# Forgetting attention as one unrolled pipeline over all heads, with keys and values turned to token order inside the input projection

## The reference, cut to what matters

```python
q, k, v, lf, xq, gate = split_fox(rmsnorm(x) @ fox_w_in, b_f)     # (2048, 8, 128) each of q, k, v
c = cumsum(lf)                                                    # per head, over tokens
s = (q_i @ k.T) * 128**-0.5 + (c_i[:, None] - c_keys[None, :])    # one block of 128 queries, causal
p = softmax(s); out = p @ v                                       # then out * silu(gate)
fox_k_prompt, fox_v_prompt = k, v in pages of 128 tokens: (16, 128, 8, 128)
```

## Time and profile before

| what | value |
|---|---|
| times of three runs | 3939.87, 3943.66, 3946.54 us |
| the profiled execution | 3935.28 us, its span 3933.8 us |
| mean granted PE clock | 0.95 of full speed |
| PE, PEld, DVE, ACT, POOL busy | 90%, 78%, 48%, 34%, 9% |
| `p00` (48 to 640 us) | 592 us |
| `p01` (640 to 1633 us) | 993 us |
| `prompt_gates` (1633 to 1662 us) | 29 us |
| `fox_attention` (1662 to 2444 us) | 782 us |
| output projection and layer 1 (2444 us on) | 1490 us |

### The profile page before, as it was taken

The page is one execution under the profiler, slowest core; times in us unless marked ns, Lnnn a source line. Parts: engine busy times, 40 slices in busy tenths (PEclk is TensorE's granted clock), DMA queues, the critical chain, the costliest instruction groups (busy, mean ns, idle before and its releaser), DMA issues. The chain is left out here.

```text
span 3933.8 us, 56268 instructions
## 1 busy us (share of the span) xinstructions
PE 3527.3 (90%) x19825; PEld 3070.0 (78%) x19825; DVE 1887.2 (48%) x3394; ACT 1333.0 (34%) x2456; POOL 338.7 (9%) x549
## 2 busy tenths in 40 slices
PE   5999998899999999688888886899499889995999
PEld 5999997788888877577777776688499878774787
DVE  3332232466666645366666665433322245565432
ACT  3112222255555534355555553111212254310111
POOL 1320000011111101001001000000000001121000
PEclk8999999999999999899999998899699999997999
DMA  3444333577777653322222222333233343565332
GB/s 120 125 124 142 115 120 90 187 234 234 228 240 240 220 167 108 105 96 96 92 93 86 86 86 63 117 113 95 87 114 118 103 128 114 168 198 186 100 113 78
DMA packets 385338, 523.96 MB, mean 133 GB/s; under 512 B 52855, under 2 KB 275064, under 8 KB 380495
## 3 DMA queue, kind: packets, MB, share of 16 engines
q1 hardware_dynamic: 317255, 398.72, 32.4%
q0 software_dynamic: 30624, 93.22, 7.1%
q10 hardware_dynamic: 37248, 29.37, 2.5%
HBM read 388.83 MB, written 132.74 MB: 133 GB/s over the span
## 5 line engine op out<-in xcount | busy, mean ns | idle before, releaser
L395 ACT ACTIVATE z_st_p<-bank 128x352 f32<-128x352 f32 (+3 forms) x325 | 168.2, 519 | 728.0 <-PE bank L378 727.3
L1518 PE MATMUL bank<-w_hi_o,b_hi_o 128*128 128x512 f32 x816 | 328.6, 403 | 69.4 <-DVE w_lo_o L1560 69.4
L378 PE MATMUL bank<-h00hi,w_hi_p 128*128 128x352 f32 x984 | 320.7, 326 | 11.4 <-DVE w_lo_p L353 7.5
L1519 PE MATMUL bank<-w_hi_o,b_lo_o 128*128 128x512 f32 x816 | 324.4, 398 | 0.0
L1520 PE MATMUL bank<-w_lo_o,b_hi_o 128*128 128x512 f32 x816 | 324.3, 397 | 0.0
L378 PE MATMUL bank<-h00hi,w_lo_p 128*128 128x352 f32 x984 | 316.9, 322 | 0.0
L378 PE MATMUL bank<-h00lo,w_hi_p 128*128 128x352 f32 x984 | 316.8, 322 | 0.0
L351 DVE CAST w_hi_p<-w_raw_p 128x1024 fp32r<-128x1024 f32 (+1 forms) x130 | 89.8, 691 | 442.8 <-PE bank L378 383.6
L378 PE MATMUL bank<-h01hi,w_hi_p 128*128 128x512 f32 x656 | 270.0, 412 | 11.6 <-DVE w_lo_p L353 11.6
L378 PE MATMUL bank<-h01lo,w_hi_p 128*128 128x512 f32 x656 | 258.4, 394 | 0.0
L378 PE MATMUL bank<-h01hi,w_lo_p 128*128 128x512 f32 x656 | 258.2, 394 | 0.0
(11 more groups left out here) (354 smaller groups left out, 8788.2 us busy)
## 6 DMA issues: line engine op xcount, KB each, us to landing
z<-z_st_p SPq DMA_DIRECT2D x128, 512.0 KB, 2.9
k_raw_sf<-in_cache_fox_k SPq DMA_DIRECT2D x128, 512.0 KB, 4.1
v_raw_sf<-in_cache_fox_v POOLq DMA_DIRECT2D x128, 512.0 KB, 4.5
w_raw_p<-in_fox_w_in SPq DMA_DIRECT2D x80, 512.0 KB, 5.4
b_raw_o<-bT SPq DMA_DIRECT2D x32, 768.0 KB, 7.3
w_raw_p<-in_pool_w_in SPq DMA_DIRECT2D x48, 512.0 KB, 5.1
out<-tok_fa ACTq DMA_DIRECT2D x64, 256.0 KB, 2.3
w_raw_o<-in_w_out ACTq DMA_DIRECT2D x24, 512.0 KB, 3.6
```

What stands on the lines that cost most here:

```text
L378: last = nc.tensor.matmul(out, wt[:, u, k, :], h[:, k, at0:at0 + width], start=(m == 0), stop=(m == MM - 1))
L395: nc.scalar.activation(z_st[0:rows, t % 2, at0:at0 + width], banks[n % 2][0:rows, 0:width], func).then_inc(z_read, 1)
L1518: nc.tensor.matmul(out, bh, w_hi[:, k, cols], start=(k == 0), stop=False)
L1519: nc.tensor.matmul(out, bl, w_hi[:, k, cols], start=False, stop=False)
```

## The change: what it does

**In the projection's passes.** The tiles of k and v come ahead of those of q. A list of jobs replaces the plain order of chunks: after the first chunk of the tile that follows a k or v tile, PE transposes the rows of the k or v tile in `z_st` into the same two PSUM banks (two jobs of 4 transposes of 128 tokens each, in `p00` a third job of one transpose for the 32 sample tokens). ACT copies them to a new buffer `tok` (three in turn) and SP stores them to the outputs. The rows of v are no longer stored to `zT`. `sample_gates` loses its transposes, copies and stores.

**In the attention.** The hardware loop over heads is gone: one list of 128 steps (`NS_`) plus 7 runs through all heads, so that step 0 of a head is the step after step 15 of the one before. q, k and v are loaded in quarters of 512 tokens (v from the output in token order, in pieces of 512 bytes) into two raw buffers each, with k's and v's halves in two buffers. The halves of a quarter of the next head (`splits`) are made in steps x with x mod 4 = 0 (q), 1 (k), 2 (v): ACT makes the hi half after the exponential of that step, DVE the lo half after `nm` and the reciprocal. The set-up of a head, its 32 transposes and its stores are gone. `sc` has 3 buffers in place of 4. Product and spread inverse of pair J share bank 6 + J mod 2, so that two pairs have banks of their own. The spread is two float32r matmuls behind the product's last one, from `dg_hi` and `dg_lo`, which POOL makes in two further operations; POOL no longer stores, SP does.

```diff
-    NT, C, Q = len(tiles), len(chunks), 4
+    jobs = []
+    for t in range(NT):
+        for ch in range(C):
+            jobs.append((t, ch, None))
+            if ch == 0 and t and tiles[t - 1][4] is not None:
+                jobs += [(t - 1, None, part) for part in token_outs[0]]
...
         def _(pe):
+                u, bank = t % 2, banks[n % 2]
+                if q == 0 and n >= 2:
+                    pe.wait_ge(z_read, n - 1)
+                if part is not None:
+                    at0, count, width = part
+                    pe.wait_ge(z_read, tile_done[t])
+                    for b in range(count):
+                        last = nc.tensor.transpose(bank[0:width, b * P:(b + 1) * P], z_st[:, u, at0 + b * P:at0 + b * P + width],
+                                                   const["ident"][:, :])
+                    last.then_inc(z_done, 1)
+                    continue
...
             def evict(n):
+                act.wait_ge(z_done, n + 1)
+                if part is not None:
+                    nc.scalar.copy(tok[0:width, m % TR, 0:count, :], bank[0:width, 0:count * P]...).then_inc(z_read, 1)
+                    return
...
-            with pe.Fori(0, FH) as h:
-                for g in range(TG):
...
+        def splits(x):
+            if x < 0:
+                return [(n, 0, ch) for ch in range(CK) for n in range(3)] if x == -1 else []
+            out = []
+            for n in range(3):
+                h, rest = divmod(x - 4 - n, NQ)
+                if rest % 4 == 0 and 1 <= h + 1 < FH:
+                    out.append((n, h + 1, rest // 4))
+            return out
...
         def _(act):
+            for x, qs, qt, _, _, _ in steps():
+                if qt is not None:
+                    ... casts of the transposed pieces to pT_hi ...
+                if qs is not None:
+                    nc.scalar.activation(sc[:, qs % NB, 0:w], sc[:, qs % NB, 0:w], ACT.Exp, ...).then_inc(p_done, 1)
+                for n, h, ch in splits(x):
+                    split(n, h, ch)          # one cast of 128x512 to the hi half, then_inc(hi_d[n], 1)
...
         def _(dve):
+            def split(n, h, ch):
+                i = CK * h + ch
+                dve.wait_ge(hi_d[n], i + 1)
+                ... one operation of 128x512 for the lo half, then_inc(lo_d[n], 1)
+            for x, qs, qt, _, jr, jm in steps():
+                ... gate and mix (jm), decay, scores and lo halves by piece, nm, reciprocal (jr): the order of before
+                for n, h, ch in splits(x):
+                    split(n, h, ch)
...
         def _(pe):
+                            if n == QB * (j + 1) - 1:
+                                last.then_inc(o_done, 1)
+                                pe.wait_ge(dgl_d, J + 1)
+                                nc.tensor.matmul(OUT[J % 2][1], ones_r[:, :], dg_hi[:, :, :]..., start=True, stop=False)
+                                nc.tensor.matmul(OUT[J % 2][1], ones_r[:, :], dg_lo[:, :, :]..., start=False, stop=True).then_inc(r_done, 1)
```

More of the change, by code:

```diff
@@ L277, in stored @@
         def stored(t):
-            return 16 * len(stores) * (t // 2 + 1)
+            return 16 * len(stores) * sum(1 for x in range(t % 2, t + 1, 2) if tiles[x][1] is not None)
         def landed(eng, t):
@@ L320, in _ @@
                 beside.advance(at)
+            for m in waiting:
+                store_tokens(m)
             store(NT - 1)
@@ L323, in _ @@
             for t in (NT - 2, NT - 1):
-                sp.wait_ge(z_out[t % 2], stored(t))
+                if stored(t):
+                    sp.wait_ge(z_out[t % 2], stored(t))
+            for u in range(TR if turned else 0):
+                sp.wait_ge(tok_out[u], 16 * len(turned[u::TR]))
         @block.gpsimd
@@ L388, in evict @@
             def evict(n):
-                t, ch = divmod(n, C)
-                func, rows = tiles[t][2:]
+                t, ch, part = jobs[n]
+                bank = banks[n % 2]
+                act.wait_ge(z_done, n + 1)
+                if part is not None:
+                    _, count, width = part
+                    m = turned.index(n)
+                    if m >= TR:
+                        act.wait_ge(tok_out[m % TR], 16 * (m // TR))
+                    nc.scalar.copy(tok[0:width, m % TR, 0:count, :], bank[0:width, 0:count * P].rearrange("p (n d) -> p n d", d=P)).then_inc(z_read, 1)
+                    return
                 at0, width = chunks[ch]
-                act.wait_ge(z_done, n + 1)
-                if ch == 0 and t >= 2:
+                if ch == 0 and t >= 2 and stored(t - 2):
                     act.wait_ge(z_out[t % 2], stored(t - 2))
[L395 to L400, removed]
+                rows_t = tiles[t][3]
+                nc.scalar.activation(z_st[0:rows_t, t % 2, at0:at0 + width], bank[0:rows_t, 0:width], tiles[t][2]).then_inc(z_read, 1)
+            for n, t, ch, part, q, at in slots():
+                if q == 0 and n:
+                    evict(n - 1)
+                if part is None:
+                    beside.advance(at)
+            evict(len(jobs) - 1)
             beside.rest()
@@ L713, in _ @@
-            for n in range(4):
-                act.wait_ge(tok_out[n], 16 * 2 * FH + 1)
+            def split(n, h, ch):
+                i = CK * h + ch
+                act.wait_ge(raw_in[n][i % 2], 16 * (i // 2 + 1))
+                if n == 0 and h:
+                    act.wait_ge(s_done, first[NQ * (h - 1) + 4 * (ch + 1)])
+                if n == 1 and h >= 2:
+                    act.wait_ge(s_done, first[NQ * (h - 1)])
+                if n == 2 and h >= 2:
+                    act.wait_ge(o_done, NCH * (h - 1))
+                nc.scalar.activation(his[n][part(n, h, ch)], raws[n][:, i % 2, :], ACT.Copy, scale=SCALE if n == 0 else 1.0).then_inc(hi_d[n], 1)
```

623 lines of the change are left out of this document (305 added, 318 removed).

## The result

The changed kernel takes 3953.19 us, the median of 18 runs (3943.75 to 3962.28), against 3944.65 us of the kernel before in the same rounds (3937.45 to 3952.02). The ratio is 1.0023, 95% interval 1.0016 to 1.0031: slower, by 6 to 12 us. The forecast was +26. The direction was right and the size was not; so the question is which terms of the sum were off, since the net is a small difference of terms of up to 107 us.

What follows compares the result with a forecast made beforehand. PE was taken to bound the projection passes, a DVE-ACT chain of waits the attention. Terms +60 −105 −22 +99 −11 +5 gave +26 on the median 3943.7: 3969 us; 80% range 3912 to 4002, the forecast's own 3945 to 3990.

Steps and rivals of the forecast that it cites:

- (c): Waits in the attention's body: banks and diagonals ready, steps 4, 7, 8, 15 shorter, −2.8 us a head; −22 us.
- Unrolling itself I put at nothing: Attention's head loop: writing it out changes no time, since the projection's code has no loop and PE runs at 99%.
- (a): Projection passes: k and v transposes between chunks, PE waiting for ACT's copies out of two banks; +60 us.
- (b): Seven borders between heads, step 15 to step 3: 20.7 us in place of 35.7; −105 us.
- (d): Splits in the attention: DVE waits for ACT's hi half behind the exponential, 1.3 or 2.1 us each; +99 us.
- (f): SBUF ports in the attention: DVE's splits slowed beside POOL's operations after steps 4, 6 and 8; +5 us.
- (e): Ends of the attention stage: shorter start before the first nm, −5, and end after the last, −6; −11 us.
- Rival B: Projection passes: the transpose jobs cost only PE's own work, 27 us; 3937 us in all, chance 0.10.
- rival C: Passes: ACT's side work delays copies in most tiles, or token stores delay paged loads; +32, 4001 us, chance 0.15.
- 0.87 + E: Attention splits: time from nm to DVE's start of the lo half, E being the exponential's length.
- Rival A: Attention: DVE's wait is slack because PE sets the step, only ACT's cast is paid; 3904 us, chance 0.20.

Runs made afterwards that it cites:

- the last two experiments: Kernel before with its head loop written out on all engines: 3911.39 us, ratio 0.9911; the same without DVE's increment of an unawaited semaphore: 3912.2 us, ratio 0.9917.
- no_turn: Changed kernel without the token transposes and their copies, all stores kept (sending zeros): 3893.86 us, ratio 0.9873 to the kernel before.
- hi_first_one_bank: hi_first with one product bank for all pairs in place of two: 3895.17 us, ratio 0.9871 to the kernel before.
- hi_first: Changed kernel with ACT making a split's hi half before the exponential of its step: 3856.0 us, ratio 0.9773 to the kernel before.

## Why the prediction was wrong in size, step by step

The step that failed is the line "Unrolling itself I put at nothing", and with it the size of term (c). Unrolling alone takes 32 us off the kernel before, and together with an unneeded increment it explains steps 8 and 12, which the forecast had nearly unchanged.

| term | forecast | measured | from |
|---|---|---|---|
| (a) transposes in the passes | +60 | +65.5 | `p00` +43.0, `p01` +22.5 |
| (b) borders | −105 | −106.6 | 251.3 to 144.7 |
| (c) waits in the body | −22 | −30.6 | last head 55.8 against 59.6, times 8 |
| (d) splits, with (f) ports | +104 | +96.8 | 543.2 − 8 × 55.8 |
| (e) ends, with the output projection's start | −11 | −14 | table; output projection 377.4 to 375.3 |
| sum | +26 | +11 | |

The sum of the measured terms, +11, agrees with the median's +8.5 (6 to 12). Of the 15 us between it and the forecast, (c) makes 9, (d) and (f) 7, (e) 3 and (b) 2, and (a) takes 5 back. The mechanisms of (a), (b), (d) and (f) hold; that of (c) was incomplete. The other misses are sizes, 2 to 7 us a term, and the larger ones fell on one side.

*(a) held.* PE's waits are 2.05 us at a plain tile of `p00` (1.99 forecast) and 1.3 to 1.6 in most of `p01` (1.34), 2.3 and 1.8 at its last two. The two late tiles of `p00` took 4.7 and 6.6, 7.2 us more than two plain ones, where 7.4 had been added. Rival B (only PE's own transposes) and rival C (late copies in most tiles, or stores that hold up the paged loads) fall with no_turn and with those rows: ACT is late at two tiles of `p00`, and at none by more than about 1 us in `p01`.

*(b) held:* 20.7 forecast, 20.7 in all seven borders. Its chain holds too: product J = 7 starts 12.6 us after `nm` of step 15 in head 2, as forecast (11.7, and 0.9 for the quarters). Of the 106.6 us some 10 are the clock: in the kernel before a border took 34.5 us where PE's granted clock was 1.00 and 35.3 to 36.8 where it was 0.86 to 0.90; in the changed kernel it is 1.00 in all seven.

*(c) failed in size,* and with it the line "Unrolling itself I put at nothing". I had argued from the projection, whose code has no loop and whose PE is 99% busy. In the attention's loop the waits on registers stand in DVE's chain: unrolling alone takes 14 us out of steps 3 to 15 (462.7 against 477.0), 14 out of the borders (which the forecast had inside its 20.7) and 2 to 3 at the ends. In the changed kernel the body's gain is 0.54 at step 4, 1.9 at step 7, 0.44 at step 8, 0.35 at step 12, 0.28 at step 15 and 0.3 over the rest; I had counted 0.5, 1.7, 0.2, none, 0.3 and none. Steps 8 and 12 are settled by the last two experiments. Step 7's 1.9 has three parts. The forecast gave it to the diagonal, the clock and the bank. About 0.8 is the clock, which did fall (granted 0.50, the 1.2 GHz level, from 1890 to 1892 us, behind two waits of PE of 1.46 and 0.81 us): in the two executions of the kernel before the step took 4.5 us in the heads where PE's granted clock stayed at 1.00 and 4.9 to 6.2 in the others. Unrolling takes 0.5 (4.47 to 3.94, both at 1.00). The last 0.6 (3.94 to 3.37) stays open. It isn't the bank, since `hi_first_one_bank` has 3.37 in its last head too. The change also moved the spread from ahead of the step's scores in PE's order to behind the product and made it float32r, and no run tests that alone.

*(d) held, 7% under.* The splits cost 1.26 to 1.27 us where 1.3 was counted (1.73 at step 5, of which 0.5 is (f)), 1.94 to 2.05 where 2.1 was, and 1.17 at the last. The first `nm` to the lo half is 1.77 us in the rows of step 5, where 0.87 + E is 1.81. Rival A (DVE's wait is slack) is refuted twice: by the last head, where steps without splits are shorter by just these amounts, and by hi_first, where the price goes when the wait goes; had PE set the step, neither could be.

*(e)* was 3 more, mostly behind the last `nm`: 8.9 less there (30.3 to 21.4), where I had 6.

*(f) held.* The timeline of the changed kernel behind the reciprocal of step 4, head 2:

```profile
1936.61 0.74 POOL L694 TENSOR_TENSOR dg_lo_fa<-dg_fa,dg_hi_fa 128x256 fp32r<-128x256 f32 x1
1936.73 1.17 DVE L801 SCALAR_TENSOR_TENSOR q_lo_fa<-q_raw_fa,q_hi_fa 128x512 fp32r<-128x512 f32 x1 [1.42 <-ACT q_hi_fa L770]
```

The lo half takes 1.17 us in place of 0.69; it begins 0.12 behind POOL's operation and ends 0.55 behind POOL's end (1937.35 to 1937.90). Of q's 32 lo halves 13 took 1.02 to 1.17 and one 0.79, 5.3 us more in all than at 0.69, where 5 were added: six behind step 4, which make step 5 longer by as much, and seven in the borders. The Trainium skill, in SBUF — State Buffer, section "SBUF: two separate sides", has such a pair exclude each other for a whole instruction; by that DVE's operation would work only from POOL's end, for some 0.6 us, and these rows agree with it.

The range, 3912 to 4002 us, held the time; the forecast's own, 3945 to 3990, held it too, at its lower end.

## What to carry to other kernels

When work is put into a pipeline's gaps, look at what stands ahead of it in the order of the engine that feeds it: here one cast behind an exponential, not before it, decided between 0.2% slower and 2.3% faster, and the wait was on DVE while the cause was ACT's order. Before a loop is unrolled, look for idle times of 0.2 to 0.4 us in the chain whose releaser is the engine's own last operation; part of them goes with the registers, and they repeat with every head. An increment that nobody waits for can be another part, though taking it out saved nothing here that shows in the whole time. Compare steps at the same granted clock before a difference is given to a bank or a wait. And where the forecast is the small difference of terms five times as large, say the range from the errors of the terms first, since 5 to 10% on each is as large as the net.

## What the runs showed of the hardware

A DVE instruction that follows a wait on DVE's own last result starts 0.37 us after it with wait values in registers and a semaphore increment ahead, 0.21 with constants, and at once (0.04) with constants and no increment. Transposes between two chunks through two banks cost 2.05 us for three jobs and 1.34 for two, of which PE works 0.96 and 0.85; behind quarters of a chunk three jobs cost 1.0, as long as ACT has no other work. A DVE operation of 128x512 with two operands in SBUF took up to 1.17 us in place of 0.69 beside POOL. In the kernel before, the same step 7 took 4.47 us at a granted PE clock of 1.00 and 6.01 at 0.72.
